# A three-block model on one core: latent heads in pairs, a reordered beginning, and three new orders of work on VectorE

## The reference

```python
# layer 0: RWKV-7 mixer
xx = shift(h) - h;  xs = h + xx * mu          # six mixes
w_log = -softplus(-(w0 + tanh(xw @ w1) @ w2)) - 0.5
a = sigmoid(a0 + (xa @ a1) @ a2)              # then r, k, v, a scan over tokens, w_o
# layer 1: latent attention, 16 heads, 64 + 32 channels for q and k, 64 for v
s = (q_nope @ k_nope + q_rope @ k_rope) * scale;  s = where(mask, s, -1e30)
o = softmax(s) @ v;  m = o @ o_w
# layer 2: grouped attention beside a two-way state-space branch
y = rms_norm((y_fwd + y_bwd + d_skip * xs) * silu(z), ssd_norm)
m = (gate_a * (attn @ w_attn) + gate_s * (y @ w_ssd)) @ w_out
# every layer
x = x + rmsnorm(m, g1);  x = x + rmsnorm(ffn(rmsnorm(x, g2)), g3)
```

## Time and profile before

| | |
|---|---|
| three runs | 1102.22, 1105.14, 1106.73 us (median 1105.14) |
| the profiled execution | 1104.69 us |
| its span, first to last instruction | 1102.7 us |
| TensorE busy | 1082.5 us, 98% of the span |
| VectorE, ScalarE, GpSimd busy | 806.1, 608.0, 210.3 us |
| granted TensorE clock, mean | 1.00 |
| TensorE's share of the chain that ended last | 79%, VectorE 10%, DMA 3%, ScalarE 3% |

### The profile page before, as it was taken

One profiled execution on the slowest core, in us unless ns is written; L12 is line 12 of the kernel. 1 busy time (PEld: TensorE's weight loads), 2 busy tenths in 40 slices (PEclk: granted clock), 3 DMA queues, 4 the chain that ended last, 5 costly groups with the idle time before them and its releaser, 6 DMA issues.

```text
span 1102.7 us, 18756 instructions
## 1 busy us (share of the span) xinstructions
PE 1082.5 (98%) x7161; PEld 939.0 (85%) x7161; DVE 806.1 (73%) x1142; ACT 608.0 (55%) x936; POOL 210.3 (19%) x230
## 2 busy tenths in 40 slices
PE   7999999999999999999999999999999999999997
PEld 6997899888888789989888888998777789888886
DVE  6997898778885658857788846688967776656543
ACT  5766355556664566846666544635665445455432
POOL 0125452112221011001222200470100001122200
PEclk9999999999999999999999999999999999999999
DMA  8553172646666556336666584556452555666552
GB/s 228 170 176 128 40 230 79 172 116 190 190 190 240 174 146 163 116 88 174 190 189 189 167 300 147 169 192 212 138 141 91 191 159 131 188 190 190 191 191 77
DMA packets 219747, 183.11 MB, mean 166 GB/s; under 512 B 43265, under 2 KB 197614, under 8 KB 219678
## 3 DMA queue, kind: packets, MB, share of 16 engines
q1 hardware_dynamic: 215566, 171.36, 52.0%
q0 software_dynamic: 3392, 8.66, 2.5%
q10 hardware_dynamic: 720, 2.13, 0.5%
HBM read 179.44 MB, written 2.69 MB: 165 GB/s over the span
## 4 chain that ended last, share of the span: by engine, by line
PE 79%; DVE 10%; DMA 3%; ACT 3%; issue 2%; POOL 1%; SPq 0%; DVEq 0%; POOLq 0%; ACTq 0%
PE bank L288 19%; PE bank L282 12%; PE bank L284 12%; PE bank L283 12%; PE bank L289 10%; PE bank L295 2%; DVE ring L413 2%; DMA ring<-in_ffn_w_out 2%; ACT arena L407 1%; PE bank L1235 1%; PE bank L1376 1%; PE bank L371 1%; DVE arena L1732 1%; DVE stat L1730 1%; PE bank L385 1%
## 5 line engine op out<-in xcount | busy, mean ns | idle before, releaser
L413 DVE TENSOR_TENSOR ring<-ring,arena 128x2048 fp32r<-128x2048 f32 (+1 forms) x136 | 306.2, 2255 | 119.8 <-ACT arena L407 118.2
L282 PE MATMUL bank<-arena 128*128 128x512 f32 (+3 forms) x980 | 343.9, 351 | 2.7 <-DVE ring L413 1.8
L288 PE MATMUL bank<-arena 128*128 128x512 f32 x960 | 337.8, 397 | 0.0
L407 ACT ACTIVATE arena<-ring 128x2048 fp32r<-128x2048 f32 (+1 forms) x143 | 268.5, 1878 | 95.2 <-DMA ring<-in_ffn_w_out 44.1
L289 PE MATMUL bank<-arena,ring 128*128 128x256 f32 x960 | 268.4, 280 | 0.0
L284 PE MATMUL bank<-arena 128*128 128x512 f32 (+3 forms) x720 | 264.8, 368 | 0.0
L288 PEld LDWEIGHTS bank<-arena 128*128 128x128 f32 x960 | 180.3, 188 | 43.7
L283 PE MATMUL bank<-ring,arena 128*128 128x512 f32 (+2 forms) x560 | 216.1, 386 | 0.0
L282 PEld LDWEIGHTS bank<-arena 128*128 128x128 f32 x980 | 185.4, 189 | 28.1 <-DVE ring L413 3.3
L289 PEld LDWEIGHTS bank<-arena,ring 128*128 128x128 f32 x960 | 181.0, 189 | 0.0
L284 PEld LDWEIGHTS bank<-arena 128*128 128x128 f32 x720 | 135.6, 188 | 22.4
(11 more groups left out here) (349 smaller groups left out, 1338.1 us busy)
## 6 DMA issues: line engine op xcount, KB each, us to landing
ring<-in_ffn_w_in SPq DMA_DIRECT2D x80, 512.0 KB, 5.0
ring<-in_ffn_w_out SPq DMA_DIRECT2D x44, 512.0 KB, 4.5
ring<-in_w_gate_up SPq DMA_DIRECT2D x40, 512.0 KB, 5.0
ring<-in_w_in SPq DMA_DIRECT2D x18, 1024.0 KB, 5.1
ring<-in_a_w_rkv SPq DMA_DIRECT2D x12, 1024.0 KB, 5.2
ring<-in_w_down SPq DMA_DIRECT2D x22, 512.0 KB, 3.7
ring<-in_a_w_o SPq DMA_DIRECT2D x4, 1024.0 KB, 9.4
arena<-in_ffn_w_in SPq DMA_DIRECT2D x8, 512.0 KB, 4.6
```

Of the source, the lines that this page charges most:

```text
L282: nc.tensor.matmul(dst, stationary[0], moving[0], start=start, stop=False)
L288: nc.tensor.matmul(dst[:, :], stationary[0], both_parts, start=start, stop=False)
L407: nc.scalar.activation(buf(hi_of(n), 0, w, arena12), ring[:, r, 0:w], ACT.Copy).then_inc(hi_ready, 1)
L413: on.tensor_tensor(ring12[:, r, 0:w], ring[:, r, 0:w], buf(hi_of(n), 0, w, arena12).bitcast(F32), ALU.subtract).then_inc(split_ready, 1)
```

## The change

On TensorE `values` goes through `by_columns`, the filler matmul ahead of `turn_p` goes, and heads 4 to 15 run in pairs: two times transposes and scores, then the values of the two heads before, with four `pt_buf` instead of two. The splits of `o_w` slots 1 to 3 leave the loop on VectorE, those of slots 2 and 3 on ScalarE, and `roped(2)` and `roped(3)` are cut in halves. At the beginning the identity is loaded first on SP instead of second on ScalarE's queue, SP waits for the first half of `x` before it loads weights, five of nine later filler matmuls go, and VectorE takes the second half's gain and `mu_w` ahead of the first half's differences. Then come the moves at the layer ends.

```diff
@@ downs_hi (and downs_lo with dve, split_dve)
             for i, (name, s) in enumerate(DOWN_SIDE):
+                if i == 2:
+                    ahead(act, LAST["ffn_out0"] - 1, split_act)
                 gained_hi(act, name, s, ...
...
@@ start_act, start_sp
             act.dma_start(x_sb[:, 0, :], A["x"][0, 0:P, :]).then_inc(x_landed[0], 16)
-            act.dma_start(cst[:, 0:P], const_dram[:, 0:P]).then_inc(const_landed, 16)
             act.dma_start(x_sb[:, 1, :], A["x"][0, P:T, :]).then_inc(x_landed[1], 16)
...
         def start_sp(sp):
+            sp.dma_start(cst[:, 0:P], const_dram[:, 0:P]).then_inc(const_landed, 16)
             rows_sp(sp, (0,), rows_landed)
+            sp.wait_ge(x_landed[0], 16)
@@ start_pe
             rows_turned(bank[0], 0).then_inc(cols_turned, 1)
-            keep_busy(pe, 3, 1)
             xn_turn(pe, 0, 0)
-            keep_busy(pe, 3, 1)
+            keep_busy(pe, 1, 1)
             xn_turn(pe, 1, 1)
             keep_busy(pe, 3, 1)
@@ start_dve
             turned_gained(0)
-            turned_out(dve, TURN_PRE0, 0)
-            nc.vector.tensor_scalar(dx[:, :, 0:1], ...
-            nc.vector.tensor_tensor(dx[:, :, 1:P], ...
             turned_gained(1)
...
                 nc.vector.tensor_tensor(mu_w[:, :, g, :], ...
+            turned_out(dve, TURN_PRE0, 0)
+            nc.vector.tensor_scalar(dx[:, :, 0:1], ...
+            nc.vector.tensor_tensor(dx[:, :, 1:P], ...
             turned_out(dve, TURN_PRE0, 1)
@@ rwkv_act
-            ahead(act, FIRST["w_k"] + 1, split_act)
             def sigmoids(bias, dst, done, base):
                 for c in range(DC):
                     if base == 0 and c == 2:
+                        ahead(act, FIRST["w_k"] + 1, split_act)
                         after_slots(act, "lora_wa2")
@@ mla_pe
             def turn_p(h):
                 if h >= 2:
                     pe.wait_ge(pt_evac, h - 1)
-                if h >= 4:
-                    keep_busy(pe, 1, 2 + h % 2, 3 * P)
...
-                nc.tensor.matmul(dst[0], pt[:, 0:P], v[:, 0, hv], start=True, stop=True)
-                nc.tensor.matmul(dst[1], pt[:, P:2 * P], v[:, 0, hv], start=True, stop=False)
-                nc.tensor.matmul(dst[1], pt[:, 2 * P:3 * P], v[:, 1, hv], start=False, stop=True).then_inc(pv_mm, 1)
+                by_columns(dst[0], pt[:, 0:P], v[:, 0, hv], True, True)
+                by_columns(dst[1], pt[:, P:2 * P], v[:, 0, hv], True, False)
+                by_columns(dst[1], pt[:, 2 * P:3 * P], v[:, 1, hv], False, True).then_inc(pv_mm, 1)
...
-            values(2)
-            for h in range(4, H):
-                turn_p(h)
-                if h + 2 < H:
-                    scores(h + 2)
-                values(h - 1)
+            for h in range(4, H, 2):
+                for x in range(2):
+                    turn_p(h + x)
+                    if h + 2 < H:
+                        scores(h + 2 + x)
+                for x in range(2):
+                    values(h - 2 + x)
                 if h == 4:
                     swapped(3)
-                if h == 11:
+                if h == 12:
                     o_turns(0)
-            values(H - 1)
+            for x in range(2):
+                values(H - 2 + x)
@@ mla_act (splits of o_w slots 2 and 3 after the last evac)
+            evac(2)
+            split_act_half(act, o_w + 1, 0)
+            exps(4)
+            evac(3)
+            exps(5)
+            for h in range(4, H - 2, 2):
+                evac(h)
+                if h == 6:
+                    split_act_half(act, o_w + 1, 1)
+                evac(h + 1)
+                exps(h + 2)
+                exps(h + 3)
+            o_hi(0)
             evac(H - 2)
             evac(H - 1)
-            emitted[act] = LAST["o_w"] + 1
+            emitted[act] = o_w + 2
+            ahead(act, LAST["o_w"], split_act)
             o_hi(1)
@@ mla_dve
             maxima(4)
-            roped(2)
             maxima(5)
+            roped(2, range(0, 2))
+            maxima(6)
+            maxima(7)
+            roped(2, range(2, 4))
             split_half(dve, o_w, 1)
...
+            split_half(dve, o_w + 1, 0)
+            o_lo(0)
+            split_half(dve, o_w + 1, 1)
+            emitted[dve] = o_w + 2
             normalized(1)
+            ahead(dve, o_w + 2, split_dve)
             o_lo(1)
+            ahead(dve, LAST["o_w"], split_dve)
@@ block_act
+            act.wait_ge(squared, 11 + NT)
             turn_act(act, TURN_SSD, 0, 0, B_SQ)
@@ block_dve
+                if a == 1:
+                    y_variance(0)
                 link(dve, op)
                 nc.vector.tensor_tensor(y[:, a, :], y[:, a, :], toks(B_Z)[:, a, :], ALU.mult).then_inc(yz_ready, 1)
...
+            y_normed(0)
+            attention_gated(0)
+            y_variance(1)
+            split_half(dve, FIRST["ssd_proj"], 1)
+            emitted[dve] = FIRST["ssd_proj"] + 1
+            y_normed(1)
             turn_dve(dve, TURN_SSD, 0, 0, B_SQ, B_SQ_LO)
...
+            mixed(0)
             ahead(dve, FIRST["w_out"], split_dve)
-            mixed(0)
```

More of the change, by code:

```diff
@@ L604, in downs_lo @@
             for i, (name, s) in enumerate(DOWN_SIDE):
+                if i == 2:
+                    ahead(dve, LAST["ffn_out0"] - 1, split_dve)
                 dve.wait_ge(xs_hi, DOWN_SPLIT0 + i + 1)
@@ L1947, in build @@
         s_buf = [buf(M_S, i * 384, (i + 1) * 384) for i in range(S_BUFS)]
-        pt_buf = [buf(M_PT, i * 384, (i + 1) * 384) for i in range(2)]
+        PT_BUFS = 4
+        pt_buf = [buf(M_PT, i * 384, (i + 1) * 384) for i in range(PT_BUFS)]
         lat_sum, lat_var, lat_rstd = small(4), small(4), small(4)
@@ L2282, in mla_act @@
             exps(3)
-            for h in range(4, H):
-                evac(h - 2)
-                exps(h)
-                if h in (4, 5):
-                    split_act_half(act, o_w + 1, h - 4)
-                if h in (6, 8):
-                    split_act_half(act, o_w + 2, h // 2 - 3)
-                if h in (10, 11):
-                    split_act_half(act, o_w + 3, h - 10)
-                if h == 13:
-                    o_hi(0)
+            evac(2)
[11 more added lines that the diff above has]
+            o_hi(0)
             evac(H - 2)
             evac(H - 1)
-            emitted[act] = LAST["o_w"] + 1
+            emitted[act] = o_w + 2
+            ahead(act, LAST["o_w"], split_act)
             o_hi(1)
@@ L2380, in q_odd_heads, with roped @@
                                         ALU.mult).then_inc(q_odd, 1)
-            def roped(s):
-                dve.wait_ge(perm_mm, Q_AT[f"p{s}"])
-                link(dve, nc.vector.tensor_tensor(q_sined[s % 2], bank[PERM_BANK[s]][:, T:2 * T], const("sinT"), ALU.mult))
-                dve.wait_ge(q_cos, s + 1)
-                for i in range(4):
+            def roped(s, heads_of=range(4)):
+                if 0 in heads_of:
+                    dve.wait_ge(perm_mm, Q_AT[f"p{s}"])
+                    link(dve, nc.vector.tensor_tensor(q_sined[s % 2], bank[PERM_BANK[s]][:, T:2 * T], const("sinT"), ALU.mult))
+                    dve.wait_ge(q_cos, s + 1)
+                for i in heads_of:
                     rows_ = slice(i * ROPE, (i + 1) * ROPE)
@@ L2429, in mla_dve @@
             maxima(4)
-            roped(2)
             maxima(5)
+            roped(2, range(0, 2))
+            maxima(6)
+            maxima(7)
+            roped(2, range(2, 4))
             split_half(dve, o_w, 1)
-            for h in range(6, H):
+            for h in range(8, H):
                 maxima(h)
-                if h == 7:
-                    roped(3)
-                if h == 6 or h == 8:
-                    split_half(dve, o_w + 1, h // 2 - 3)
-                if h in (9, 10):
-                    split_half(dve, o_w + 2, h - 9)
+                if h == 9:
+                    roped(3, range(0, 2))
                 if h == 11:
+                    roped(3, range(2, 4))
+                if h == 13:
                     normalized(0)
-                if h in (12, 13):
-                    split_half(dve, o_w + 3, h - 12)
-                if h == 14:
-                    o_lo(0)
-            emitted[dve] = LAST["o_w"] + 1
+            split_half(dve, o_w + 1, 0)
+            o_lo(0)
+            split_half(dve, o_w + 1, 1)
+            emitted[dve] = o_w + 2
             normalized(1)
+            ahead(dve, o_w + 2, split_dve)
             o_lo(1)
+            ahead(dve, LAST["o_w"], split_dve)
             early_lo(dve, 1, 0)
```

21 lines of the change are left out of this document (8 added, 13 removed).

## The result

The changed kernel takes **1096.28 us** (median of 4 runs, 1094.72 to 1096.76), the kernel before, run beside it, 1104.8: a ratio of 0.9923, 95% interval 0.9904 to 0.9942. The forecast was 1096.5. The profiled execution took 1096.36, its span is 1094.2.

The account below looks back on a forecast made before the run. TensorE, busy 98%, bounds the kernel: only fewer or shorter matmuls or its few waits can help. Terms 1.6 + 1.3 + 4.2 + 1.3 = 8.4 off 1104.69 give 1096.3, 1096.7 against the median; forecast 1096.5 us, range 1093.0 to 1101.0.

Parts of the forecast that it names:

- Beginning: Start of the kernel to the second mix: reordered loads, fillers and VectorE work gain 1.6 us, upper bound 2.4.
- so the 0.7 goes: Beginning: VectorE's 0.70 us wait for ScalarE at 30.56 vanishes once the split stands behind two of eight sigmoids.
- 0.9 counts and 2.3 doesn't: Beginning: the chain downstream is VectorE's, so its 0.9 us lead counts and TensorE's 2.3 us earlier L1169 doesn't.
- The held-back weights: Beginning: weights issued some 1.4 us later on SP cost nothing, with 2.7 us of cover; without cover the term is 0.
- End of the first FFN: Near 380 us: ring-slot splits moved ahead remove TensorE's whole wait, gaining 1.3 us, lower bound 0.7.
- Latent heads: Second mixer's head loop: 5.3 us less TensorE work, less new waits, nets 4.2 us, from 2.5 to 5.9.
- The form: Head loop: values by columns save 0.28 us a pair, 2.0 for seven pairs; no gain for single heads.
- a ring of 2.9: Head loop: transposes, copy, exponentials and transposes again form a hand-off chain of 2.9 us a pair against TensorE's 3.0.
- the rival of the hand-offs: Head loop: hand-offs govern, each pair waits, heads gain only 2.0 us, total 1098.7; chance 15%.
- The two rules: Head loop: 2x for 64 columns would give 4.6 instead of 2.0; clock swings from short idle spells speak against removing fillers.
- End of the third mixer: Waits of 1.2 and 0.6 us go, 0.5 returns at w_out slot 2: 1.3 us net, from 0.6 to 1.9.
- yn and the gating are both ready at about 856.1, when TensorE comes: Third mixer's end: with split and gating no longer ahead of the first L3145, TensorE's 1.2 us wait goes.

Follow-up runs that it names:

- e11: Changed kernel with both batches of three fillers around the first transposes and ScalarE's early split of the second w_k slot put back; 1095.86 us, one execution.
- e9: Kernel before with the head loop's twelve filler matmuls taken out, heads still one by one; 1103.24 us, one execution.
- e6: Changed kernel with the latent heads' values as plain matmuls instead of by_columns, still in pairs with four buffers; 1094.70 us.
- e12: e8 with a single 128-column matmul added ahead of every fourth channel tile in each FFN loop; 1099.84 us against 1102.32, ratio 0.9978.
- e5: The changed kernel itself run once more, nothing altered; 1094.47 us against 1102.81, ratio 0.9933.
- e7: Changed kernel with the filler matmul ahead of each transposed head put back from head 4 on; 1095.87 us.
- e8: Changed kernel with three more VectorE moves: rotary rows before maxima(7), gating before scaled y, half a w_out split before mixed(0); 1090.50 us against 1102.81, ratio 0.989.

## Why the prediction was right, and where it wasn't

- **The total** was right to 0.2 us, the sum of 8.4 against 8.3 to 8.5 measured. Part of that is luck. The two profiled executions drew one fast pace each, in different FFNs; with another draw the same code would read 2 us off. And the terms' errors met: the four stretches gained 1.6, 1.7, 4.4 and 0.55, 8.2 in all, so 0.6 more than laid out in two of them hides 0.75 less in the last. I took one execution's time as a base that is good to 0.45 us; it is good to about 3.
- **Beginning: right in size, half wrong in its pieces.** 1.6 laid out, 1.6 to 1.7 measured. L1169 starts at 12.45 (12.2 forecast), VectorE's second L1143 at 28.98 (29.0), without a wait for ScalarE. The first mix starts 0.82 earlier (16.75 to 15.93) where I had 0.9; the fillers alone are worth 1.08 there (e11). The step that failed is "so the 0.7 goes" by the moved split: e11 puts the split back and only 0.1 returns. The rest, 0.66, came from the step that I had ruled out, "0.9 counts and 2.3 doesn't": part of TensorE's lead did count, since ScalarE had waited for its L1172. The held-back weights cost nothing, as costed. One reading was off: the clock didn't rise after "some 4 us". The fillers start at 5.11, and the matmuls' starts go from 0.21 us apart to 0.11 only at 10.2.
- **End of the first FFN: right mechanism, unstable size.** I said 1.3, "the whole wait". The wait of that execution cost 1.7, for the view lists 0.3 too little, and those of four others 0.9 to 1.0. A wait on a landing, read once, is one draw.
- **Latent heads: 4.2 laid out, 4.4 measured; the working was off twice and the errors met.** The form gave 1.8 (2.0 laid out), at 0.29 a pair. The fillers gave 1.9, not 3.4. The 0.28 each was read from a loop in which they partly filled the single heads' hand-offs (e9: 0.5 without them). In turn 0.7 remain for the pairs and the moved work, where I had them only as a cost of 1.1 in waits. Those came as 0.86 at the permutation and 0.46 and 0.31 at two transposes, 1.6 in all. Steady pairs take 2.98 against TensorE's own 3.0 that I had laid beside a ring of 2.9, with no wait listed, so the rival of the hand-offs fell, barely. Everything moved behind the loop was hidden: no wait in `o_w`.
- **The two rules.** The Trainium skill's up to 2x for 64 moving columns (TensorEngine Tiling (Array Packing), "Theoretical Speedup") would, by an estimate, have made e6 4.6 us slower in its pairs; it lost 1.8. Its "Key Properties", a drain when the mode changes, fits the 0.09 ahead of and the late start behind each group. Of the swing that the Trainium skill, TensorE: Matmul & The Clock Gate, "A second HAM failure mode", reports, nothing shows: the granted clock is 1.00 over gaps up to 0.86 in the loop. That doesn't make fillers useless everywhere: it did fall behind the one gap of 2.79 us, in e12.
- **End of the third mixer: wrong, 1.3 laid out and 0.55 measured.** The step that failed is "yn and the gating are both ready at about 856.1, when TensorE comes". I moved the scaled `y` forward and did not ask for its own input, GpSimd's root, which lets it start 0.54 us after VectorE is free; the gating behind is then 0.74 late. The second new wait, for `w_out` slot 2, was foreseen at 0.5 and is 0.80.

## What to carry to other kernels

When an item is moved up on an engine's list, follow its own inputs too: the wait goes to whatever stands behind it. Here swapping two calls and filling an idle 5.9 us with half a split brought back 1.4 us. Price a filler by the loop without it, not by its duration, and a new form together with the order that shares its fixed cost. Terms of 1 to 2 us in a kernel of 1,100 are told by one instruction's start in both traces, stretch by stretch; the medians of four runs each couldn't rank e5, e6 and e7. Look behind a long wait too: in e12 the slow clock added 1.6 us to a wait of 2.8.

## What was not expected of the hardware

- Matmul pairs of 512 and 256 columns (type float32r, one pass each) run at 0.3466 or 0.3533 us a pair at the same granted clock, never idle, and keep it for a whole loop; a single 128-column matmul (float32, two passes) between them switched it 8 times in 15, in one execution. With three such loops a program's time spreads over some 6 us: the kernel before took 1100.62 to 1106.53 in 30 runs.
- The same ring slot landed 3.6, 5.0 or 6.2 us behind the one ahead of it in three executions (e8, e7, e12), by the start of ScalarE's copy. In e12 that was worth 4.4 us of TensorE: 2.8 of waiting and 1.6 of the clock at 0.50 behind it.
